# Down projection of a gated-MLP block: one weight sum moved to VectorE, partial results accumulated in DRAM, transfers and products reordered

## What is computed

```python
h2 = rmsnorm(x, ffn_pre_g)
up = causal_depthwise_conv(h2 @ w_up, conv_f_w, conv_f_b)
u_gate, u_val = jnp.split(up, 2, axis=-1)
f = (jax.nn.gelu(u_gate, approximate=True) * u_val) @ w_down      # (512 x 5632) @ (5632 x 2048)
x = x + rmsnorm(f, ffn_post_g)
e = (p[i] @ w_ple) * jax.nn.sigmoid(x @ w_ple_gate)
x = x + rmsnorm(e, ple_post_g)
```

## Time and profile before

| what | value |
|---|---|
| runs of the kernel, median of 3 | 2586.01 us (2580.02 to 2586.61) |
| the profiled execution's own time | 2584.03 us |
| its span, first to last instruction | 2582.2 us |
| mean granted TensorE clock | 0.993 |
| TensorE busy | 2523.4 us, 98% |
| VectorE busy | 1805.8 us, 70% |
| ScalarE busy | 1019.7 us, 39% |
| moved by DMA | 432.35 MB, mean 167 GB/s |

### The profile page before, as it was taken

One profiled execution on the slowest core, in us unless ns is written; L12 is line 12 of the kernel. 1 busy time (PEld: TensorE's weight loads), 2 busy tenths in 40 slices (PEclk: granted clock), 3 DMA queues, 4 the chain that ended last, 5 costly groups with the idle time before them and its releaser, 6 DMA issues. The chain is left out here.

```text
span 2582.2 us, 36184 instructions
## 1 busy us (share of the span) xinstructions
PE 2523.4 (98%) x14322; PEld 2218.1 (86%) x14322; DVE 1805.8 (70%) x2194; ACT 1019.7 (39%) x1188; POOL 207.8 (8%) x291
## 2 busy tenths in 40 slices
PE   8999999999999999999999999999999999898998
PEld 7888888888888888799999999999987788676886
DVE  5888766653334236889989999899987776677534
ACT  5222322252223224444444444444454444445323
POOL 0000000000000000011110111111120111310000
PEclk9999999999999999999999999999999999999999
DMA  5333333333333323477777777777796988985221
GB/s 164 104 97 98 98 98 98 90 114 98 98 98 130 126 96 137 143 200 205 213 193 218 207 206 215 202 201 216 203 320 199 293 261 251 329 205 214 96 98 66
DMA packets 258798, 432.35 MB, mean 167 GB/s; under 512 B 13236, under 2 KB 162396, under 8 KB 257628
## 3 DMA queue, kind: packets, MB, share of 16 engines
q1 hardware_dynamic: 220480, 291.54, 33.9%
q0 software_dynamic: 35248, 134.23, 21.7%
q10 hardware_dynamic: 2924, 4.54, 0.5%
HBM read 393.30 MB, written 36.96 MB: 167 GB/s over the span
## 5 line engine op out<-in xcount | busy, mean ns | idle before, releaser
L1023 ACT ACTIVATE w_hi<-ring_raw 128x1024 fp32r<-128x1024 f32 x426 | 450.3, 1059 | 603.7 <-PE ps L926 387.5
L1429 DVE TENSOR_TENSOR ring_lo<-ring_raw,w_hi 128x1024 fp32r<-128x1024 f32 x426 | 518.9, 1221 | 221.8 <-ACT w_hi L1023 220.2
L1418 DVE TENSOR_TENSOR w_lo<-w_raw,w_hi 128x1024 fp32r<-128x1024 f32 x194 | 236.8, 1223 | 408.8 <-ACT w_hi L1013 408.5
L1013 ACT ACTIVATE w_hi<-w_raw 128x1024 fp32r<-128x1024 f32 x194 | 204.9, 1059 | 527.3 <-PE ps L717 387.1
L715 PE MATMUL ps<-xg_hi,w_hi 128*128 128x512 f32 x1024 | 400.7, 391 | 0.7 <-DVE w_lo L1418 0.6
L717 PE MATMUL ps<-xg_hi,w_lo 128*128 128x512 f32 x1024 | 399.2, 390 | 0.0
L716 PE MATMUL ps<-xg_lo,w_hi 128*128 128x512 f32 x1024 | 399.1, 390 | 0.0
L924 PE MATMUL ps<-s_hi,w_hi 128*128 128x256 f32 x1280 | 362.2, 283 | 3.2 <-issue 3.2
L926 PE MATMUL ps<-s_hi,ring_lo 128*128 128x256 f32 x1280 | 362.2, 283 | 0.0
L925 PE MATMUL ps<-s_lo,w_hi 128*128 128x256 f32 x1280 | 361.8, 283 | 0.0
L924 PE MATMUL ps<-xg_hi,w_hi 128*128 128x256 f32 x960 | 271.0, 282 | 0.4 <-DVE ring_lo L1429 0.4
(11 more groups left out here) (242 smaller groups left out, 4199.0 us busy)
## 6 DMA issues: line engine op xcount, KB each, us to landing
ring_raw<-in_w_up SPq DMA_DIRECT2D x200, 512.0 KB, 4.9
w_raw<-in_w_in SPq DMA_DIRECT2D x112, 512.0 KB, 3.8
ring_raw<-in_w_down SPq DMA_DIRECT2D x110, 512.0 KB, 7.2
ring_raw<-in_w_up POOLq DMA_DIRECT2D x80, 512.0 KB, 6.2
ring_raw<-in_w_down POOLq DMA_DIRECT2D x44, 512.0 KB, 8.7
w_raw<-in_w_o SPq DMA_DIRECT2D x32, 512.0 KB, 3.6
ring_raw<-in_w_ple_gate SPq DMA_DIRECT2D x32, 512.0 KB, 3.6
xd_raw<-gx_dram POOLq DMA_DIRECT2D x14, 1024.0 KB, 11.3
```

What stands on the lines that cost most here:

```text
L1023: f(w_hi[:, (U_S + n) % SLOTS], raw_of(n), ACT.Copy).then_inc(hi_ready, 1)
L1418: dve.tensor_tensor(w_lo[:, s], w_raw[:, u.slot(RAW)], as_f32(w_hi[:, s]), ALU.subtract).then_inc(lo_ready, 1)
L1429: dve.tensor_tensor(low_of_unit(n), raw_of(n), as_f32(w_hi[:, (U_S + n) % SLOTS]), ALU.subtract).then_inc(lo_ready, 1)
```

## The change

- T1's sum: from pair 1 on, the accumulating transfer for T1 is gone. VectorE adds W11's block (still raw in its ring buffer) to T1's loaded block, in a new `first_down`, just ahead of W11's low half. Pair 0 keeps the transfer for T1, and T3 keeps it everywhere.
- Partial results: there is one `part_dram` for both passes. Pass 0 stores to it, pass 1 stores with an accumulating transfer (SBUF to DRAM), and `part_in` reads the sum back. The 8 transfers of `part_added` are gone.
- Order: in all pairs but the first, W11, W22, T1, T2 go group by group. In pairs with four groups the tail has T3 and W21/T4 mixed, with T3 at positions 16, 17, 20, 23 and W21's first unit at 18.
- Transfers: `load_blocks`, `part_in`, the loads of `x3` and the last parameter loads are issued at other positions, and `PREPARED` follows.

```diff
-def pair_units(quads):
-    units = [(W11, q) for q in range(quads)]
-    units += [(mat, q) for q in range(quads) for mat in (W22, T1, T2)]
-    units += [(T3, q) for q in range(quads)]
-    return units + [(mat, q) for q in range(quads) for mat in (W21, T4)]
+def pair_units(p, h):
+    quads = PASSES[p]
+    if p + h == 0:
+        units = [(W11, q) for q in range(quads)]
+        units += [(mat, q) for q in range(quads) for mat in (W22, T1, T2)]
+    else:
+        units = [(mat, q) for q in range(quads) for mat in (W11, W22, T1, T2)]
+    if quads < 4:
+        return units + [(T3, q) for q in range(quads)] + [(mat, q) for q in range(quads) for mat in (W21, T4)]
+    return units + [(T3, 0), (T3, 1), (W21, 0), (T4, 0), (T3, 2), (W21, 3), (T4, 3), (T3, 3), (W21, 1), (T4, 1), (W21, 2), (T4, 2)]
...
+def bounds(p, h, mat):
+    at = [k for k, (m, _) in enumerate(pair_units(p, h)) if m == mat]
+    return at[0], at[-1]
...
 def adds(n):
-    return 1 if mat_of(n) in (T1, T3) else 0
+    return 1 if mat_of(n) == T3 or mat_of(n) == T1 and n < N_DOWN + START(0, 1) else 0
+def is_sum(n):
+    return mat_of(n) in (T2, T4) or mat_of(n) == T1 and n >= N_DOWN + START(0, 1)
...
-            PREPARED.update({at + 10: (p + 1, W11), at + 19: (p + 1, W22)})
-            PREPARED.update({at + 21: (1, T1), at + 23: (1, T2), at + 30: (1, T3)} if p == 0 else
-                            {at + 25: (2, T1), at + 29: (2, T2), at + 32: (2, T3)})
-            PREPARED.update({at + 34: (p + 1, W21), at + 36: (p + 1, T4)})
+            PREPARED.update({at + 18: (p + 1, W11), at + 20: (p + 1, W22)})
+            PREPARED.update({at + 22: (1, T1), at + 24: (1, T2), at + 37: (1, T3)} if p == 0 else
+                            {at + 25: (2, T1), at + 26: (2, T2), at + 35: (2, T3)})
+            PREPARED.update({at + 39: (p + 1, W21), at + 41: (p + 1, T4)} if p == 0 else {at + 37: (2, W21), at + 39: (2, T4)})
...
             def store_part(p, h, k):
+                to = part_dram[h, k].rearrange("p (a f) -> p a f", a=2)
+                if p == 0:
+                    pool.dma_start(to, cb[buffer][:]).then_inc(c_out[buffer], 16)
+                else:
+                    pool.wait_ge(c_out[buffer], 16 * (h + 1))
+                    pool.dma_start(to, cb[buffer][:], accum_op=ALU.add).then_inc(c_out[buffer], 16)
...
-                if i == 0:
-                    load_blocks(0, W21)
-                    load_blocks(0, T4)
-                if i == 7:
+                if i == 6:
                     pool.wait_ge(gx_out[0], g_stored(QUADS - 1))
                     load_blocks(0, T3)
+                if i == 8:
+                    load_blocks(0, W21)
+                if i == 10:
+                    load_blocks(0, T4)
                 if h == 1 and nxt < len(PASSES):
-                    if at == quads - 1:
+                    if at == bounds(p, h, W11)[1]:
                         load_blocks(nxt, W11)
...
-                    if at == 5 * quads - 1:
-                        if spread_pieces(nxt, T1):
-                            load_blocks(nxt, T1)
-                        load_blocks(nxt, T3)
-                    if at == 7 * quads - 1:
-                        if spread_pieces(nxt, T2):
-                            load_blocks(nxt, T2)
-                        load_blocks(nxt, W21)
-                        load_blocks(nxt, T4)
+                    if at == bounds(p, h, T3)[1] and spread_pieces(nxt, T1):
+                        load_blocks(nxt, T1)
+                        load_blocks(nxt, T2)
+                if h == 0 and p > 0:
+                    if at == 1:
+                        load_blocks(p, T3)
+                    if at == 3:
+                        load_blocks(p, W21)
+                    if at == 5:
+                        load_blocks(p, T4)
...
+                for k in range(4):
+                    if i == START(1, 1) + 17 + 3 * k:
+                        part_in(0, k)
+                    if i == START(2) + 6 + 3 * k:
+                        part_in(1, k)
...
+            def first_down(n):
+                dve.wait_ge(ring_in[SLOT[n]], landed(n))
+                dve.wait_ge(ring_in[SLOT[n + 2]], landed(n + 2))
+                dve.wait_ge(units_done, U_S + PREVIOUS[n + 2] + 1)
+                dve.tensor_tensor(raw_of(n + 2), raw_of(n + 2), raw_of(n), ALU.add).then_inc(sum_ready, 1)
...
-                if at == 5 * quads - 1:
+                if at == bounds(p, h, T3)[1]:
                     take_third(pair)
```

More of the change, by code:

```diff
@@ L162, in sums_made @@
 def sums_made(n):
-    return sum(1 for m in range(n + 1) if mat_of(m) in (T2, T4))
+    return sum(1 for m in range(n + 1) if is_sum(m))
 class At:
@@ L612, in add_down @@
             def add_down(i):
-                if i < len(DOWN) and DOWN[i][2] in (T1, T3):
+                if i < len(DOWN) and adds(N_DOWN + i):
                     p, h, mat, q = DOWN[i]
@@ L684, in _ @@
                     store_part((pair - 1) // 2, (pair - 1) % 2, 2)
[L685 to L693, removed]
+                for k in range(4):
[3 more added lines that the diff above has]
+                        part_in(1, k)
+                if i == START(2, 1) + 11:
                     pool.wait_ge(x2_out, 16)
-                    for n in range(NG):
-                        pool.dma_start(x3[:, n], x2_dram[:, n]).then_inc(x2_in[n], 16)
+                if i >= START(2, 1) + 12 and i < START(2, 1) + 14 or i > START(2, 1) + 14 and i <= START(2, 1) + 16:
+                    n = i - START(2, 1) - 12 - (1 if i > START(2, 1) + 14 else 0)
+                    pool.dma_start(x3[:, n], x2_dram[:, n]).then_inc(x2_in[n], 16)
                 if i == START(2, 1) + 14:
+                    pool.dma_start(p_raw[:], p_t.rearrange("(k q) t -> q k t", q=P)).then_inc(p_in, 16)
                     pool.dma_start(gain_f[:], on_all(ffn_post_g)).then_inc(gain_f_in, 16)
-                    pool.dma_start(p_raw[:], p_t.rearrange("(k q) t -> q k t", q=P)).then_inc(p_in, 16)
             pool.wait_ge(units_done, U_G)
@@ L952, in down @@
                 n, g = N_DOWN + i, PRODUCTS * (2 * p + h) + ORDER.index(mat)
-                if q == 0:
+                ends = bounds(p, h, mat)
+                first, final = i - START(p, h) == ends[0], i - START(p, h) == ends[1]
+                if first:
                     slot_free(g)
@@ L959, in down @@
                 s, w_low = (U_S + n) % SLOTS, low_of_unit(n)
-                first, final = q == 0, q == PASSES[p] - 1
                 for k in range(2):
@@ L1015, in split_ring @@
             def split_ring(n):
[L1017 removed]
+                if is_sum(n):
                     act.wait_ge(sum_ready, sums_made(n))
@@ L1420, in split_ring @@
             def split_ring(n):
+                if n >= N_DOWN + START(0, 1) and mat_of(n) == W11:
+                    first_down(n)
                 if n >= N_DOWN and mat_of(n) == W22:
@@ L1444, in fourth_down @@
                 dve.wait_ge(ring_in[SLOT[n]], landed(n))
-                dve.wait_ge(sum_ready, sums_made(n + 1) - 1)
+                q = DOWN[n - N_DOWN][3]
+                dve.wait_ge(sum_ready, sums_made(max(m for m in range(N_DOWN, n) if mat_of(m) == T2 and DOWN[m - N_DOWN][3] == q)))
                 dve.tensor_tensor(raw_of(n + 1), raw_of(n + 1), raw_of(n), ALU.add).then_inc(sum_ready, 1)
```

38 lines of the change are left out of this document (17 added, 21 removed).

## The result

The changed kernel takes **2594.91 us** (median of 8 runs, 2590.01 to 2596.13), the kernel before 2584.59 (8 runs, 2580.02 to 2586.75). The ratio is 1.0035, with a 95% interval of 1.0026 to 1.0045: slower by 9 us by this ratio, 10 between the medians. The forecast was 2583.2 with a range to 2592.0, so the result lies outside it, on the slower side. The profiled execution took 2590.78, against 2584.03 for the one of before, +6.75 us.

What follows compares the result with a forecast made beforehand. It took TensorE, busy 98%, as the bound, so only its waits or low clock could be won. Idle -1.9 us and clock +1.1, together -0.8 on the profiled 2584.0, gave 2583.2 us, range 2568 to 2592.

Steps and rivals of the forecast that it cites:

- a trade: Down stage: TensorE's waits change place, idle 27.2 against 29.1 us; 2579 to 2592 us, chance 0.57.
- the timetable: W21's first unit: take_first ends after its banks are due; waits 2.2, 2.8, 2.2 us in pairs 1 to 3.
- The rival that T1's sum comes late: VectorE waits in first_down for T1's load, 1 us a group with slow loads; chance 0.02 beyond the trade's range.
- pair 4's term: W21's first unit in pair 4: wait of 2.3 us, 2.8 with the third T3 transfer a little late.
- pair 0's term: W21's first unit in pair 0: wait of 8.5 us instead of 4.87, bounds 5.7 and 18.
- The 8.2 us that I let stand: Down stage: the part of 29.1 us idle put down to stage start, pair 5 and hand-over, taken as unchanged.
- the new terms: Down stage: new idle time, 8.5 + 2.7 + 2.8 + 2.2 + 2.8 = 19.0 us.
- its 3.4 us for the throttled time: Waits after the change: extra loss if low clock inside waits counts too, by the skill's rule; result 2582.0.
- The cost of accumulating into DRAM: GpSimd's queue: eight accumulating stores replace plain stores and part_added; cost 0, bounds 0 and 3 us.
- The clock term: Lower clock behind waits in the down stage: 6.2 us lost after the change against 5.1 before, +1.1.
- The new wait is not there: Faster rival: W21's banks free in pairs 1 to 4, 2568.2 us, or waits without low clock, 2575.9; chance 0.33.
- T3 behind the inputs: Slower rival: T3 transfers in pairs 0 and 1 land late behind 1 MB input blocks; 2600 us, chance 0.08.

Runs made afterwards that it cites:

- Experiment 6: Changed kernel with pair 4's T4 input block issued at position 7 instead of 5 and split at 13 instead of 11: 2588.83 us, ratio 1.0011.
- experiment 3: Changed kernel with pass 1's stores plain instead of accumulating, leaving out pass 0's partial results: 2589.87 us, ratio 1.0013.
- Experiment 2: Changed kernel with pair 0's input blocks of W21 and T4 issued at position 0, not 8 and 10: 2589.72 us, ratio 1.0013.
- experiment 1: Changed kernel with take_second and take_first of pairs 0 to 3 put at position 15, ahead of VectorE's low half: 2581.52 us, ratio 0.9984.
- 8: Changed kernel with five edits: takes early everywhere, stored-part additions later, pair 0's inputs at position 0, T1's next-pass block later, pair 4's T4 block later: 2571.8 us.
- experiment 7: Kernel before the change, with take_second and take_first of pairs 0 to 3 ahead of VectorE's low half at the last T2 position: 2574.63 us, ratio 0.9962.
- 9: Changed kernel with the five edits of 8, and pair 4's T4 block split at position 12 instead of 13: 2568.97 us, ratio 0.993.

## Why the prediction was wrong

**What held.** The forecast was a trade: low halves of pair 4 go, waits for L2025's successor come at W21's first unit in pairs 0 to 4. That is what the trace shows (one low half of 1.95 us stays), and the timetable worked out from the code and three durations hit pairs 1, 2, 3 and 5 to 0.2 us. The 9.48 us wait is gone. The only wait near the 18 sums is the 1.18 us at the border of pairs 1 and 2, where I had added 0.5 for VectorE's 38 us of work; what part of it they cost is not shown. The rival that T1's sum comes late is dead, since no sum had idle time ahead of it.

**The step that failed: pair 4's term, "2.8 with its third T3 transfer a little late".** It measured 8.75, 6 us more. From the `part_added` being gone and the inputs no longer in one burst I had concluded that the queue is in time, and never counted what does stand on it: eight transfers at 3.8 us each are 30 us, and the first can't be issued before VectorE has made the last products of pair 3 ready (L2077). The rate was in my own rows, 3.84 us for an accumulating transfer. I used it for T3's two in a row, and let blocks and stores pass for free. Experiment 6 takes one of the eight from ahead of T3's third, and its 1.75 us on VectorE from ahead of the take-outs, and 3.5 to 3.9 us come back; experiment 3 makes two of them cheaper, and 2.8 come back. My own sign for it ("a transfer to land in under 12 us around the start of pair 4") failed with 15.3 us, and so did the one on low halves in pair 4 (1.95 us, not under 1).

**The same fault in pair 0's term, 8.5.** It measured 12.2. The length of VectorE's chain was right: it is 16.4 us from ScalarE's start on T3's second unit (1949.0) to the end of L2055 (1965.4), and I had 16.6. But I let it begin with the end of position 13 and made only the third transfer late, while the second landed at 1948.9. I priced a transfer's lateness by what is ahead of it in one place only. Experiment 2 shows that the inputs' new positions, which I blamed, are worth 2 us of this. The order of the takes is worth more: experiment 1 took 5.4 us from it (12.2 to 6.7), and with both edits (8) 3.4 are left. The sign that I had named for this (T3's units in pair 0 later than four units ahead of use) came true, on the second unit and not the third.

**A reading of the rows that was incomplete.** The 8.2 us that I let stand were put down to the start of the stage, pair 5 and the hand-over, which are 6.2. The other 2.1 are two waits for low halves in pair 0, 0.36 and 1.70 us, ahead of the ones that I listed; after the change 0.75 is left of them. So the new terms together came to 28.9 us and not 19.0, and 1.3 us won where I had counted on nothing hide part of that. Nor does the working say how it comes to its 3.4 us for the throttled time in the waits after the change.

**The cost of accumulating into DRAM**, which I took as 0 with bounds 0 and 3, measured 5.6 us to land against 3.8, and 2.8 us of pair 4's wait: within the bounds, at the upper end, and my reason for zero (who waits for the data has 40 us) looked at the wrong party. Those who wait are the transfers queued behind it.

**The clock term, +1.1.** Of the four new dips that I gave a chance of two thirds each, the first profile of the changed kernel shows one, behind pair 4's 6.80 us (granted clock 0.53 from 2285.3 to 2291.3), and none behind the waits of 2.02, 2.75 and 2.08; the second shows three. The first also has one at the start of the stage (0.60 from 1901 to 1905), behind a wait of 2.6 us that has none in the trace of before. Its busy time in the stage grew by 1.2 us, so the size of the term came out right (+1.1 forecast) by luck: the dip at the start of the stage adds to it, pair 4 has one dip where before it had two, and pairs 1 to 3, where I had put most of it, have none. Six of the other seven runs of the changed kernel take 2594.5 to 2596.1 us, some 4 to 5 over that first profile, at a mean granted clock of 0.989 to 0.991, where that profile has 0.991. Clock dips are the likely cause, but these runs have no trace and it isn't shown. By the rule of the Trainium skill (TensorE: Matmul & The Clock Gate, Terms), which counts the whole throttled time, the result was to be 2582.0. The miss of 12 us lies elsewhere and doesn't decide between that rule and mine.

**The rivals.** "The new wait is not there" is refuted, 2.0 to 2.8 us in three pairs. "T3 behind the inputs" named the right mechanism, late T3 transfers, on the right side, with a chance of 0.08. But it put the decision in pair 1, where T3's fourth transfer took 18.0 us (past my 17), and missed pair 4. In pair 1 VectorE waited 1.59 us for it and then had no gap until the low half that came 1.18 us late, so it cost no more than that. It was the better story, and underrated because I read 8.7 us, a median over the stage, as if it spoke for its busiest stretch, beside a row of 23.4.

**One reading was wrong although it did no harm.** The 0.97 and 0.73 of pair 1 in the kernel before I put down to late T3 units; experiment 7 removes both by moving the takes. A low half that ends a wait can be late because the take-out ahead of it on the same engine was.

What stays open: whether pair 0 can be had without its 2 to 3 us (in 9 it has 0.77, 2.06 and 2.64), and why one execution lowers its clock behind a wait of 2 us and the next does not, what sets the pitch of the queue, and which part of the gain in 6 is the queue's.

## What to carry to other kernels

Count a queue as you count an engine: list every transfer in it in order, stores and input blocks too, give each the pitch that the trace shows for its size and kind in a busy stretch, and see when the one that matters lands; a median over a stage doesn't say that. When a step is moved earlier on one engine, move what frees its buffers as well: here the take-outs stood behind work that waited for late transfers, so that each late transfer was paid twice, and placing them first gave 0.4% in the kernel before and 0.5% in the changed one, while the change itself lost 0.35%. And before a change adds a new way to do a sum, look at what the old trace would gain from the order alone: experiment 7 is a few lines and 0.4%.

## What the hardware showed that I had not expected

- In its busy stretches, with SyncE's loads on the same DMA engines, GpSimd's queue landed plain transfers of 512, 768 and 1024 KB 2.5, 3.8 and 5.1 us apart, and accumulating ones of 512 KB, stores to DRAM and weight loads alike, 3.5 to 3.9. So an accumulating transfer took the queue as long as a plain one of half as many bytes again.
- An accumulating store of 512 KB from SBUF to DRAM landed in 5.6 us, a plain one at the same place in 3.8 (medians of three).
- The same wait of 2.02 us, in the same kernel, is followed by a granted clock of 1.00 in one execution and 0.58 in the next.
